# Final rows of an encoder step: half of the column tiles transposed between the last products, each row tile stored in two halves

## What is computed

```python
    x = x + (jax.nn.silu(g_conv) * (h2 @ w_up)) @ w_down
...
def rmsnorm(x, g):
    x32 = x.astype(jnp.float32)
    y = x32 * lax.rsqrt(jnp.mean(x32 * x32, axis=-1, keepdims=True) + EPS)
    return y.astype(x.dtype) * g
...
    y_prompt = rmsnorm(xp, norm_final)
    y_sample = rmsnorm(xs, norm_final)
```

## Time and profile before

| | us |
|---|---|
| Median of 3 runs | 1749.39 |
| Lowest and highest run | 1749.38, 1750.65 |
| Span of the profiled execution | 1748.6 |
| PE busy | 1717.8 (98%) |
| DVE busy | 1341.5 (77%) |
| ACT busy | 757.8 (43%) |
| POOL busy | 579.4 (33%) |

### The profile page before, as it was taken

The page is one execution under the profiler, slowest core; times in us unless marked ns, Lnnn a source line. Parts: engine busy times, 40 slices in busy tenths (PEclk is TensorE's granted clock), DMA queues, the critical chain, the costliest instruction groups (busy, mean ns, idle before and its releaser), DMA issues.

```text
span 1748.6 us, 32318 instructions
## 1 busy us (share of the span) xinstructions
PE 1717.8 (98%) x12275; PEld 1678.6 (96%) x12275; DVE 1341.5 (77%) x2193; ACT 757.8 (43%) x1333; POOL 579.4 (33%) x466
## 2 busy tenths in 40 slices
PE   6999999999999999999999999999999999999998
PEld 6999999999999999888899999999999999999998
DVE  6689899978799996778759989666666665865765
ACT  5344333368621234767734563333333333422334
POOL 2211842266745431000021102655455554121130
PEclk9999999999999999999999999999999999999999
DMA  4101111111243415422324112222222223533112
GB/s 157 49 25 43 49 43 48 49 38 28 68 137 124 128 40 171 144 85 85 109 71 151 49 49 61 87 85 75 74 80 80 87 74 111 167 117 112 61 37 100
DMA packets 179190, 146.43 MB, mean 84 GB/s; under 512 B 10140, under 2 KB 149676, under 8 KB 179052
## 3 DMA queue, kind: packets, MB, share of 16 engines
q1 hardware_dynamic: 178076, 142.54, 26.3%
q0 software_dynamic: 976, 2.00, 0.5%
HBM read 118.22 MB, written 26.28 MB: 83 GB/s over the span
## 4 chain that ended last, share of the span: by engine, by line
PE 91%; DVE 4%; ACT 2%; issue 1%; DMA 1%; POOL 1%; SPq 0%; DVEq 0%; ACTq 0%; POOLq 0%
PE ps L1602 28%; PE ps L2079 23%; PE ps L2152 7%; PE ps L2138 7%; PE ps L1714 5%; PE ps L1775 4%; PE ps L1795 4%; PE ps L1614 4%; PE ps L2009 3%; PE ps L1921 3%; PE ps L1869 1%; PE ps L1632 1%; PE ps L1876 1%; ACT probs L2537 0%; DMA x_rows<-in_x_prompt 0%
## 5 line engine op out<-in xcount | busy, mean ns | idle before, releaser
L3171 DVE MAX8 top<-key_mask 128x8 f32<-128x1024 f32 (+5 forms) x166 | 151.8, 917 | 9.7 <-DVE key_mask L3171 3.4
L1602 PE MATMUL ps<-h_hi,w_hi 128*128 128x352 f32 (+1 forms) x720 | 158.0, 327 | 0.0
L1602 PE MATMUL ps<-h_hi,w_lo 128*128 128x352 f32 (+1 forms) x720 | 155.2, 323 | 0.0
L1602 PE MATMUL ps<-h_lo,w_hi 128*128 128x352 f32 (+1 forms) x720 | 154.8, 323 | 0.0
L1289 POOL TENSOR_TENSOR w_lo<-w_raw,w_hi 128x512 fp32r<-128x512 f32 (+1 forms) x43 | 79.3, 1843 | 217.4 <-ACT w_hi L2240 217.3
L3171 DVE MATCH_REPLACE8 key_mask<-top,key_mask 128x1024 f32<-128x1024 f32 (+5 forms) x166 | 149.4, 904 | 0.3 <-issue 0.3
L2079 PE MATMUL ps<-mix_hi,quarter_hi 128*128 128x264 f32 x672 | 136.9, 285 | 0.2 <-ACT x_one L2240 0.2
L2079 PE MATMUL ps<-mix_hi,quarter_lo 128*128 128x264 f32 x672 | 136.4, 284 | 0.0
L2079 PE MATMUL ps<-mix_lo,quarter_hi 128*128 128x264 f32 x672 | 136.0, 284 | 0.0
L1602 PEld LDWEIGHTS ps<-h_hi,w_hi 128*128 128x128 f32 (+1 forms) x720 | 120.6, 187 | 2.6 <-issue 0.9
L1602 PEld LDWEIGHTS ps<-h_hi,w_lo 128*128 128x128 f32 (+1 forms) x720 | 122.5, 186 | 0.5
(11 more groups left out here) (452 smaller groups left out, 5017.5 us busy)
## 6 DMA issues: line engine op xcount, KB each, us to landing
w_raw<-in_w_in SPq DMA_DIRECT2D x54, 256.0 KB, 3.0
w_hi<-gate_highs SPq DMA_DIRECT2D x48, 256.0 KB, 2.8
w_lo<-gate_lows SPq DMA_DIRECT2D x48, 256.0 KB, 3.0
ffn_tiles<-t SPq DMA_DIRECT2D x44, 264.0 KB, 2.4
w_raw<-in_w_gate SPq DMA_DIRECT2D x44, 256.0 KB, 3.1
w_raw<-in_w_up SPq DMA_DIRECT2D x44, 256.0 KB, 3.1
w_raw_in_lo<-in_w_in SPq DMA_DIRECT2D x30, 256.0 KB, 3.0
w_raw<-in_w_down SPq DMA_DIRECT2D x32, 192.0 KB, 2.8
```

Source lines behind the costliest of these rows:

```text
L1602: last = nc.tensor.matmul(PS[0:rows, NB * k + b, 0:e - a], w[:, k, t, 0:rows], x[:, t, a:e], start=m == 0 and w is WHI and x is hi, stop=m ...
L3171: step.mark(V_.max(top, s) if find else V_.match_replace(s, top, s, TAKEN))
```

## The change

Nine groups of four transposes are put between products of the last two pairs (`first_halves`, places in the table `FIRST_HALVES`): they turn column tiles 0 to 3 of each row tile into one PSUM bank, 2 or 3 by turns. ACT copies each bank unscaled to a new SBUF tile `y_first_half` (`first_half`). When a set's scales are there, DVE multiplies these halves from SBUF into `Y` (`y_halves`). At the end PE transposes only column tiles 4 to 7 into one bank per row tile (six banks take turns), and ACT (seven row tiles) or DVE (8 and 4) scales 512 columns. SP stores each half of a row tile by its own transfer. Three semaphores of the start are used again: `half_t` is `x_in5`, `half_out` is `x_in6` and `half_scaled` is `x_in7`; each starts from 16, so that `landed(n)` is 16 + n.

```diff
+        half_t, half_out, half_scaled = x_in[5:8]
...
-        Y_BY = {5: "act", 6: "dve", 7: "act", 8: "dve", 0: "act", 1: "dve", 2: "act", 3: "dve", 4: "act"}
+        Y_BY = {5: "act", 6: "act", 7: "act", 8: "dve", 0: "act", 1: "act", 2: "act", 3: "act", 4: "dve"}
...
+        def y_bank(i):
+            return (0, 1, 2, 3, 6, 7, 0, 1, 2)[Y_ORDER.index(i)]
...
+        FIRST_HALVES = {(2 * PAIRS - 2, 4): [0], (2 * PAIRS - 2, 5): [1], (2 * PAIRS - 2, 6): [2],
+                        (2 * PAIRS - 1, 0): [3, 4], (2 * PAIRS - 1, 1): [5, 6], (2 * PAIRS - 1, 2): [7],
+                        (2 * PAIRS - 1, 3): [8]}
...
-            for i in Y_ORDER:
-                eng, count = y_count(i)
-                sp.wait_ge(y_ready[eng], count)
-                out = outs[0][0, i * P:(i + 1) * P, :] if i < NT else outs[1][0]
-                sp.dma_start(out, Y[0:rows_of(i), i, :]).then_inc(y_out, 16)
-            sp.wait_ge(y_out, 16 * (NT + 1))
...
+            for rows in (Y_ORDER[:len(LATE_ROWS)], Y_ORDER[len(LATE_ROWS):]):
+                for i in rows:
+                    sp.wait_ge(half_scaled, landed(Y_ORDER.index(i) + 1))
+                    sp.dma_start(out_rows(i)[:, 0:KH * P], Y[0:rows_of(i), i, 0:KH * P]).then_inc(y_out, 16)
+                for i in rows:
+                    eng, count = y_count(i)
+                    sp.wait_ge(y_ready[eng], count)
+                    sp.dma_start(out_rows(i)[:, KH * P:D], Y[0:rows_of(i), i, KH * P:D]).then_inc(y_out, 16)
+            sp.wait_ge(y_out, 32 * (NT + 1))
...
                     pair_product(m, Q_A11, *mixed(0), True, lambda s, t: (b_ready, whole_count(s, t, 0)))
+                    first_halves(m, 0)
...
+                    if m == 2 * PAIRS - 1:
+                        pe.wait_ge(half_out, landed(NT + 1))
                     pair_product(m, Q_A12, *second(0), True)
+                    first_halves(m, 5)
...
+            def first_halves(m, after):
+
+                for i in FIRST_HALVES.get((m, after), ()):
+                    r = rows_of(i)
+                    pe.wait_ge(y_columns, KH)
+                    pe.wait_ge(added, pair_count(2 * PAIRS - 3, Q_A22))
+                    if i >= 2:
+                        pe.wait_ge(half_out, landed(i - 1))
+                    for j in range(KH):
+                        transpose(PS[0:r, 2 + i % 2, j * P:(j + 1) * P], xg(j)[:, i * P:i * P + r],
+                                  half_t if j == KH - 1 else None)
...
+            def first_half(i):
+                r = rows_of(i)
+                act.wait_ge(half_t, landed(i + 1))
+                copy(half_row(i), PS[0:r, 2 + i % 2, :]).then_inc(half_out, 1)
...
                         if i % 2 == 0:
...
                             square(j)
                         else:
                             column(j)
+                    if m == 2 * PAIRS - 1 and 0 < i < 5:
+                        for row in FIRST_HALVES[m, i - 1]:
+                            first_half(row)
...
-                nc.scalar.activation(Y[0:rows_of(i), i, :], y_banks(i), ACT.Copy,
+                nc.scalar.activation(Y[0:rows_of(i), i, KH * P:D], y_banks(i), ACT.Copy,
...
+            def y_halves(i):
+                r = rows_of(i)
+                dve.wait_ge(y_rstd, 1 if i in LATE_ROWS else 2)
+                V_.tensor_scalar(Y[0:r, i, 0:KH * P], half_row(i), ss[0:r, 2, i:i + 1], None,
+                                 ALU.mult).then_inc(half_scaled, 1)
```

More of the change, by code:

```diff
@@ L374, in build @@
         STATES = place("state_rows_out", [P, P], F32, 22, 3 * 4 * KH * P)
+        Y_HALF = place("y_first_half", [P, NT, KH * P], F32, 0)
+        Y_HALF_S = place("y_first_half_sample", [P, KH * P], F32, 22, 2048)
         F_OUT = nc.dram_tensor("ffn_tiles", (FT, P, TOK), F32, kind="Internal").ap()
@@ L798, in build, with half_row @@
         A11, A12, A21, A22 = (quarter_of(h, part) for h in range(2) for part in range(2))
-        Y_BY = {5: "act", 6: "dve", 7: "act", 8: "dve", 0: "act", 1: "dve", 2: "act", 3: "dve", 4: "act"}
+        Y_BY = {5: "act", 6: "act", 7: "act", 8: "dve", 0: "act", 1: "act", 2: "act", 3: "act", 4: "dve"}
         Y_ORDER = list(Y_BY)
         assert sorted(Y_ORDER) == sorted((*LATE_ROWS, *EARLY_ROWS)) and set(Y_ORDER[:len(LATE_ROWS)]) == set(LATE_ROWS)
+        def y_bank(i):
+            return (0, 1, 2, 3, 6, 7, 0, 1, 2)[Y_ORDER.index(i)]
         def y_banks(i):
-            first = (0, 2, 6)[Y_ORDER.index(i) % 3]
-            return PS[0:rows_of(i), first:first + 2, :].rearrange("p b n -> p (b n)")
+            return PS[0:rows_of(i), y_bank(i), :]
+        def half_row(i):
+            return Y_HALF[:, i, :] if i < NT else Y_HALF_S[0:DEC, :]
+        FIRST_HALVES = {(2 * PAIRS - 2, 4): [0], (2 * PAIRS - 2, 5): [1], (2 * PAIRS - 2, 6): [2],
+                        (2 * PAIRS - 1, 0): [3, 4], (2 * PAIRS - 1, 1): [5, 6], (2 * PAIRS - 1, 2): [7],
+                        (2 * PAIRS - 1, 3): [8]}
         def y_count(i):
@@ L2196, in down_pairs @@
                                  late_sums if m == 2 * PAIRS - 1 else None)
+                    first_halves(m, 6)
+            def first_halves(m, after):
[8 more added lines that the diff above has]
+                                  half_t if j == KH - 1 else None)
             def late_sums():
@@ L2210, in y_rows @@
                 n, r = Y_ORDER.index(i), rows_of(i)
-                first = (0, 2, 6)[n % 3]
-                if n >= 3:
-                    eng, count = y_count(Y_ORDER[n - 3])
+                if n in (2, 3):
+                    pe.wait_ge(added, pair_count(2 * PAIRS - 1, Q_A12))
+                elif n in (4, 5):
+                    pe.wait_ge(added, pair_count(2 * PAIRS - 1, Q_A22))
+                elif n >= 6:
+                    eng, count = y_count(Y_ORDER[n - 6])
                     pe.wait_ge(y_ready[eng], count)
-                for j in range(KT):
-                    transpose(PS[0:r, first + j // 4, (j % 4) * P:(j % 4 + 1) * P],
+                for j in range(KH, KT):
+                    transpose(PS[0:r, y_bank(i), (j - KH) * P:(j - KH + 1) * P],
                               xg(j)[:, i * P:i * P + r], y_t if j == KT - 1 else None)
@@ L2225, in _ @@
             y_rows(Y_ORDER[0])
+            y_rows(Y_ORDER[1])
             pe.wait_ge(ssq_sum, 2 * KT + 3)
             row_sums(SSQ, EARLY_ROWS, 5, last=False)
+            y_rows(Y_ORDER[2])
             pe.wait_ge(res_sq, 2 * KT + 2)
             row_sums(SQ_LAST, EARLY_ROWS, 5, first=False).then_inc(y_sums, 1)
-            pe.wait_ge(added, pair_count(2 * PAIRS - 1, Q_A22))
-            for i in Y_ORDER[1:]:
-                if i == EARLY_ROWS[0]:
-                    pe.wait_ge(y_columns, KT + 2)
+            y_rows(Y_ORDER[3])
+            pe.wait_ge(y_columns, KT + 2)
+            for i in Y_ORDER[4:]:
                 y_rows(i)
@@ L2919, in _ @@
                         pair_high(m + 1, q)
+                    for row in FIRST_HALVES.get((m, i), ()) if m < 2 * PAIRS - 1 else ():
+                        first_half(row)
                     if m > PAIRS and i < 4:
@@ L4094, in _ @@
                              ALU.mult).then_inc(y_columns, 1)
+            dve.wait_ge(half_out, landed(NT + 1))
+            for i in Y_ORDER[:len(LATE_ROWS)]:
+                y_halves(i)
             dve.wait_ge(y_sums, 2)
@@ L4097, in _ @@
             late, early = ([i for i in rows if Y_BY[i] == "dve"] for rows in (Y_ORDER[:len(LATE_ROWS)], Y_ORDER[len(LATE_ROWS):]))
-            y_rows(late[0])
+            for i in late:
+                y_rows(i)
             scales(EARLY_ROWS, 2)
-            for i in (*late[1:], *early):
+            for i in Y_ORDER[len(LATE_ROWS):]:
+                y_halves(i)
+            for i in early:
                 y_rows(i)
```

8 lines of the change are left out of this document (7 added, 1 removed).

## The result

The changed kernel takes 1753.59 us (median of 20 runs, 1752.43 to 1755.73) against 1750.45 for the kernel before in the same session (20 runs, 1749.28 to 1752.01). The ratio is 1.0018, with a 95% interval from 1.0012 to 1.0024, so 3.1 us slower (2.1 to 4.2). The prediction was 1750.9 with a range up to 1753.4, and +1.5 us. The sign of the sum was right and its size was not; the time lies 0.2 us above the range. The median of before was itself 1.1 us above the 1749.39 on which the forecast stood, so only the difference is argued with from here on.

The account below looks back on a forecast made before the run. PE bounds the kernel up to the last product, then the transfers bound the tail. Groups +3.9, wait +0.7 and tail -3.1 make +1.5 us on 1749.4: 1750.9 us, range 1749.3 to 1753.4.

Parts of the forecast that it names:

- The groups: +3.9: Nine groups of four transposes between PE's last products, 0.44 us each, nothing covering them: +3.9 us.
- The wait at row 7: +0.7: PE waits before row 7's group for ACT's copy of row 5, which stands behind ACT's second squares: +0.7 us.
- E: End of the last product, at the first final transpose: 1729.49 before, forecast 4.6 us later at 1734.1.
- Rivals 1 and 4: 1: no wait at row 7, 1750.2 us, chance 0.22; 4: groups partly hidden in PE's stream, 1748.3 us, chance 0.05.
- The clock: PE's clock with transposes and an idle wait among the last products: expected to stay full, nothing charged.
- rival 3: PE's clock falls in the last products; two low spells add 3.2 us, giving 1754.1 us; chance 0.09.
- The early rows' scaling: In the tail, DVE's first early half scaled at E + 6.9, after its refinements end at E + 6.4.
- Rival 5: DVE's nine more scalings delay early rows, transfers run dry 1 to 2 us: 1752 us; inside the forecast's 0.50.
- So the transfers run without a gap from E + 3.7 ... 10.7 us, to E + 14.4 ... -3.1 us.: Tail: 4.33 MB of stores flow unbroken, end at E + 16.0 against E + 19.1, giving back 3.1 us.
- 0.33 us or so each: Time SP was taken to spend issuing each store in the tail.
- The rate: Tail stores taken to move at 404 GB/s; 0.3 us for shorter rows in halves left to the range.
- Rival 2: Stores in halves run slower, at 350 GB/s: 4.33 MB take 12.4 us, +1.7, 1752.6 us; chance 0.14.

Follow-up runs that it names:

- the run with the fetch on the first store of before: The kernel before with the late rows' row sums done seven times over (24 products more): 1757.76 us, 1.0045.

## Why the prediction was wrong

Point by point, in the order of its steps:

- **The groups: +3.9.** Right: 35.57 - 31.64 = 3.93 without the wait (copies ahead of the square), at a granted clock of 1.00.
- **The wait at row 7: +0.7.** Right in place, cause and size: 0.66 of idle time, 0.87 when its cause is taken away. E came 4.8 later for a forecast of 4.6. Rivals 1 and 4 fall.
- **The clock.** Right to charge nothing. It stood at 1.00 up to E with nine groups and the idle 0.66 between products, so rival 3 falls, and with it the rule of the Trainium skill (TensorE: Matmul & The Clock Gate, Part 4: PE-mode transpose), which isn't borne out for short groups among products.
- **The early rows' scaling.** First half begun at E + 6.1, forecast E + 6.4. The first store's issue began at E + 2.7, forecast 2.8. Rival 5 falls: what ran dry, ran dry with scaled halves waiting in SBUF.
- **"So the transfers run without a gap from E + 3.7 ... 10.7 us, to E + 14.4 ... -3.1 us."** This is the step that failed. The transfers had a gap, from E + 5.0 to E + 6.1. The issue behind which it lies took 2.20 us where the working took "0.33 us or so each". With the fetch moved away the tail is 16.17, so the change gives back 2.91 (forecast 3.1), and the hold takes 1.57 of it (0.6 to 1.6 over the three executions). The sum is then +4.80 - 2.91 + 1.57 = +3.46 by the profile, +3.1 by the medians. Without the hold it would have been +1.9, near the +1.5. Of the 2.7 us by which the time lies above 1750.9, 1.1 is the later session's median of before and 1.6 is the change's own; with the earlier base the time would have been near 1752.5, inside the range with the step as wrong as it is.
- **The rate.** Forecast 404 GB/s; measured 376 to 384 at full share, in halves and in whole stores. For 4.33 MB that is up to 0.8 us more. It doesn't show in the tail's length: with the fetch moved away 99% of the bytes were through at E + 15.2, where the working had E + 14.4, but only 1.0 us passed from there to the end of the span, where I had put 1.6 (and the last packet ends 0.8 before it). Two errors of nearly one size; that the 16.0 and the 16.17 agree so well is in part luck. Rival 2 (350 GB/s, +3.2) came nearest in the difference, +3.1, for a reason that isn't its own: halves cost some 0.2 us here. In the kernel before they cost 0.73 together with an issue of 1.12 us. The specifications of the Trainium skill (DMA: Bandwidth & Descriptors, Specifications) give about 358 GB/s as the HBM limit per core, half of what two cores share. Only one core runs here, and the windows of 6 us and more at full share, 376 to 404, are over that, so this figure wasn't what bound the stores.

The warning was in the profile of before. The row from which I took 0.33 has a greatest value of 723, and over the whole program single issues of 1.0 to 1.8 us occur. I read the median of nine issues and didn't ask what the long ones elsewhere have beside them. A count over all issues of SP in the changed kernel's execution: of 33 that overlap a fetch, 13 took over 1 us; of 517 that don't, 3. Before: 10 of 30, and 3 of 511. A long issue is likelier to overlap something, and with whole stores the tail has long issues without a fetch, so the count alone proves nothing. With the two pairs of runs in which only repeated transposes moved the fetch (third issue 2.20 to 0.45, and 1.66 to 0.51), and the six traces against five, the cause is shown for the early stores of this tail.

**What stays open.** How the fetch holds the issue. Where no store's data was in flight the fetch took 0.96 us and held nothing (the run with the fetch on the first store of before); beside 0.35 to 0.5 MB of stores it took 0.96 to 1.8, and the issue begun around its start, or the one next to it, took 1.1 to 2.2, but for the kernel before. That one had an issue of 0.33 us in the midst of a fetch of 1.67, begun 0.7 behind its start, and in three of the runs the issue at the very start of a fetch was short and the one after it held. So the meeting isn't sufficient, and it is needed only for the early stores, as late ones take 1.1 to 1.4 us without it, and whether the fetch holds the issue, or both are held by the data of the earlier stores, wasn't told apart. The Trainium skill (Runtime: NRT & Kernel Launch, Instruction fetch mechanics) says that the sequencer fetches the next 16 KiB by itself and that the cost is mostly hidden. For PE, whose program it is, the trace agrees, with no idle time at 1739.46; the price was paid by SP.

## What to carry to other kernels

When the bound moves from one engine to the transfers, what stands on the busy engine is paid in full (0.44 us for each group of four transposes here), while the tail gives back no more than its idle transfers: nine groups cost 3.9 (and 0.9 of wait) for 2.9 given back, and that only with the hold away; four cost 1.8 for 1.7. Count both before moving work out of a tail. And where a tail lives from the queue of a few stores, take the greatest duration of an issue elsewhere in the program, not the median, and look at what runs beside it; a fetch of code is placed by the count of instructions ahead of it (in all fourteen traces the last one starts behind 12,236 to 12,273 recorded weight loads of PE, wherever these fall in time), so an edit to that engine's program can put one on a store or take it off. With more data issued ahead the hold cost less: some 0.25 to 0.8 us with whole row tiles, 0.6 to 1.6 with halves.

## What the runs showed of the hardware that I had not expected

- A 16,384-byte fetch of PE's code at the time of the early stores went, in six traces of six, with an issue of SP of 1.3 to 2.2 us in place of 0.45 to 0.83, and moving it away took 0.6 to 1.6 us off the tail with stores in halves. With no store in flight the fetch takes 0.96 us.
- SP's issue of a whole row tile took 0.33 to 0.36 us at first, and up to 1.2 to 1.4 us with several queued ahead of it and no fetch.
- 64 idle instructions in the program, in two places, didn't move the fetch (the traces don't list them); 24 transposes did, from E + 3.6 to E - 0.4.
- In the run with the row sums done nine times over, PE was busy without a break (11.20 of 11.20 us, by ends that are modelled) with products of one column, and its granted clock fell from 1.00 to 0.50, the level of 1.2 GHz, and stood there for over 10 us more, through full products and transposes. In the changed kernel 36 transposes between the products didn't lower it. The Trainium skill (TensorE: Matmul & The Clock Gate, Why this matters for your kernels) advises keeping the engine busy continuously to get to the full clock; in that row it was kept busy and the clock fell, and the measurement decides.
